# Merging input projection and recurrence preparation, with the convolution as matmuls and modulation by contraction quarters

## The reference, cut to what matters

```
# block 1
u = rmsnorm(x) * gain * (1 + sc_mix) + sh_mix
p = u @ w_in                                   # 2816 columns = 22 tiles of 128
y = p[:, 0:512] * sigmoid(p[:, 512:1024])      # tiles 0-3 and 4-7
y_conv = silu(layernorm(causal_depthwise_conv31(y) + b))
xs = p_r + mu * (shift_by_one(p_r) - p_r)      # the other 14 tiles: r, k, v (4 each), w|a, g
decay, a, gate = low-rank products of xs[w], xs[a], xs[g] with sigmoids
y_rwkv = recurrence(r, k, v, decay, a)         # 8 heads of 64, a state of 64 x 64 each
x += gt_mix * (concat(y_conv, y_rwkv) @ w_out)
x += gt_ffn * peer_ffn(modulated norm of x)    # top-16 of 16384 experts, 8 heads: row gather
x = rmsnorm(x)
# block 2: modulated norm, projections, two attentions, output, gated FFN
```

## Time and profile before

| | us |
|---|---|
| median of 3 runs | 1514.3 (1513.95 to 1515.32) |
| profiled execution | 1514.75 |
| its span, first to last instruction | 1512.5 |
| PE busy | 1257.1 (83%) |
| VectorE busy | 944.1 (62%) |
| ScalarE busy | 424.7 (28%) |
| input projection and convolution, 33 to 133 | PE 85.4, VectorE 74.7, ScalarE 30.5 busy |

### The profile page before, as it was taken

One profiled execution on the slowest core, in us unless ns is written; L12 is line 12 of the kernel. 1 busy time (PEld: TensorE's weight loads), 2 busy tenths in 40 slices (PEclk: granted clock), 3 DMA queues, 4 the chain that ended last, 5 costly groups with the idle time before them and its releaser, 6 DMA issues. The chain is left out here.

```text
span 1512.5 us, 19714 instructions
## 1 busy us (share of the span) xinstructions
PE 1257.1 (83%) x7650; PEld 860.7 (57%) x7650; DVE 944.1 (62%) x2121; ACT 424.7 (28%) x883; POOL 278.0 (18%) x263
## 2 busy tenths in 40 slices
PE   4996897784888788888888777887999778799988
PEld 2984585573424243333333222236998658799988
DVE  1696433347969787877878786567343867555443
ACT  3314222452111111111101010016355163544331
POOL 0000000002444444443434434310000000000000
PEclk8997898787999999999999999998999899899999
DMA  9545833843999999999999999974553034354443
GB/s 399 205 172 224 358 137 121 361 160 139 421 422 422 421 421 421 422 420 420 414 421 409 422 420 412 421 322 201 197 209 112 1 119 165 112 203 183 173 162 140
DMA packets 48188, 426.68 MB, mean 282 GB/s; under 512 B 5344, under 2 KB 5472, under 8 KB 5600
## 3 DMA queue, kind: packets, MB, share of 16 engines
q0 software_dynamic: 36864, 268.45, 42.9%
q1 hardware_dynamic: 11232, 156.98, 26.9%
HBM read 424.36 MB, written 1.05 MB: 281 GB/s over the span
## 5 line engine op out<-in xcount | busy, mean ns | idle before, releaser
L1298 PE MATMUL bank<-arena 128*128 128x512 f32 x1024 | 499.1, 615 | 129.5 <-DVE arena L1441 129.2
L1298 PEld LDWEIGHTS bank<-arena 128*128 128x128 f32 x1024 | 176.6, 190 | 437.0 <-DVE arena L1441 285.8
L1479 DVE CUSTOM_DVE_ANT_0 arena<-arena 128x1024 f32<-128x1024 f32 x256 | 313.5, 1224 | 149.3 <-DMA arena<-experts_in,arena 145.0
L1225 POOL DMA_INDIRECT arena<-experts_in,arena x256 | 277.4, 1084 | 589.5 <-PE bank L1298 349.9
L467 PE MATMUL bank<-rounded,rounded 128*128 128x256 f32 x1144 | 335.0, 293 | 44.5 <-DVE rounded L430 36.3
L469 PE MATMUL bank<-rounded,ring_r 128*128 128x256 f32 x1144 | 328.5, 287 | 0.0
L468 PE MATMUL bank<-rounded,rounded 128*128 128x256 f32 x1144 | 327.3, 286 | 0.0
L444 DVE TENSOR_TENSOR ring_r<-ring,rounded 128x1024 fp32r<-128x1024 f32 (+2 forms) x137 | 171.8, 1267 | 142.5 <-ACT rounded L439 142.4
L467 PEld LDWEIGHTS bank<-rounded,rounded 128*128 128x128 f32 x1144 | 222.7, 195 | 49.0 <-issue 27.8
L468 PEld LDWEIGHTS bank<-rounded,rounded 128*128 128x128 f32 x1144 | 223.9, 196 | 3.0 <-issue 2.9
L469 PEld LDWEIGHTS bank<-rounded,ring_r 128*128 128x128 f32 x1144 | 223.4, 195 | 0.0
(11 more groups left out here) (255 smaller groups left out, 993.8 us busy)
## 6 DMA issues: line engine op xcount, KB each, us to landing
ring<-slots_in SPq DMA_DIRECT2D x73, 2048.0 KB, 8.5
arena<-experts_in,arena POOLq DMA_INDIRECT x256, 13.6
xT<-xT_in SPq DMA_DIRECT2D x1, 1024.0 KB, 10.7
mixT<-slots_in SPq DMA_DIRECT2D x1, 1024.0 KB, 6.4
out_dram<-xT SPq DMA_DIRECT2D x1, 1024.0 KB, 3.9
con<-consts_in SPq DMA_DIRECT2D x1, 552.0 KB, 8.7
vec<-vecs_in SPq DMA_DIRECT2D x1, 167.0 KB, 2.3
```

The source lines that it names most:

```text
L1225: pool.indirect_dma_start(rows[:, r % GRING, :], None, experts_in, bass.IndirectOffsetOnAxis(ap=expert[:, tt, at:at + 1], axis=0)).then_in ...
L1298: ins = pe.matmul(psum[2 * tt + half][:, :], diag[:, r % DIAGS, :], rows[:, r % GRING, D + 512 * half:D + 512 * half + 512], start=(h == 0 ...
L1479: dve.tensor_tensor_reduce(rows[:, r % GRING, 0:D], rows[:, r % GRING, 0:D], utok[:, tt, :], 1.0, 0.0, ALU.mult, ALU.add, hdot[:, r:r + 1] ...
```

## The change

The order of the slots changes, and block 2's modulation leaves the recurrence. Old and new:

```
- ("ada", 4), ("w_in", 6), ("ada2", 2), ("lora", 1), ("ada3", 6), ("mod2", 12), ("w_out", 2), ("w_q", 4),
- ("w_in2", 10), ("rope", 1), ("gates", 2), ("w_br", 2), ...
+ ("ada", 4), ("w_in", 1), ("lora", 1), ("w_in_b", 5), ("convw", 1), ("ada_b", 8), ("w_out", 2), ("w_q", 4),
+ ("w_in2", 10), ("gates", 1), ("mod2b", 4), ("gates_b", 1), ("mod2c", 4), ("w_br", 2), ...
+ KEYS_AT, ROPE_AT, EARLY_ROWS = NSLOTS, NSLOTS + 1, NSLOTS + 2
```

**Modulation.** A slot now holds a quarter of the contraction (256 rows) for 2048 columns; six groups. `pe_mod(pe, g, first, last)` does the slices k from first to last:

```
+ for k in range(first, last):
+     ...
+     for j in range(4):
+         ins = pe.matmul(psum[MOD_BANK[g]][32 * j:32 * j + 32, :], csil[:, which, k, :],
+                         w[:, 2048 * (k % 2) + 512 * j:2048 * (k % 2) + 512 * j + 512],
+                         start=(k == 0), stop=(k == KT - 1))
+     if k % 2: ...            # frees the slot
+ def pe_mod_cols(pe, g):      # 4 products for 2048 columns, a 4-column piece of the identity as moving operand
```

**One block for projection and preparation.** The 14 recurrence tiles come first, in the order w|a, g, k, r, v, and are split (`buffers=4`); then b and a, plain. The preparation's steps are set between:

```
+ ORDER_IN = (12, 13, 4, 5, 6, 7, 0, 1, 2, 3, 8, 9, 10, 11)
+ if i == 4: lora_products()       # PE, after tile i
+ elif i == 6: gate_products()
+ elif i == 8: ... head_sums(5, bv, rw["ss"])
+ elif i == 15: ... head_sums(3, T2, rw["bonus"])

+ win.dve_lo(dve, 5)               # VectorE
+ win.dve_lo(dve, 6)
+ dve.wait_ge(rw["sigw"], CT)
+ for ct in range(CT): dve.tensor_tensor_scan(T3[:, ct, :], ...)
+ win.dve_lo(dve, 7)
+ shift(4, 6, 4)
+ win.dve_lo(dve, 8)
+ shift(6, 8, 6)
+ ...
```

**Convolution.** In the recurrence block SyncE first copies `ypad` to four time-shifted copies in SBUF (24 transfers, rows of 284 elements): partitions 32 b + ch of channel group b at shifts 0 to 3. A new slot `convw` holds diagonal weights. For each channel tile 32 products, two times between the steps of chunk 2, two times of chunk 3; ScalarE evicts with the bias:

```
+ for r in range(8):
+     for b in range(4):
+         ins = pe.matmul(psum[6 + ct % 2][32 * b:32 * b + 32, 0:T], w[:, b, ct, r, :],
+                         taps(b, ct)[:, 4 * r:4 * r + T], start=(r == 0), stop=(r == 7))
```

More of the change, by code:

```diff
@@ new lines, in build, with pe_mod @@
+        EARLY_AT = ARENA - GRING * 2 * D
+        early = area(EARLY_AT, 4, SLOT)
+        mrow = area(ARENA - 512, 512)
+        mrow_early = area(10752, 512)
+        def pe_mod(pe, g, first, last):
+            which, slots = GV[g]
+            for k in range(first, last):
+                if slots is None:
+                    if k % 2 == 0:
+                        pe.wait_ge(early_loaded[k // 2], 16)
+                    w = early[:, k // 2, :]
+                else:
+                    if k % 2 == 0:
+                        wait_slot(pe, slots[k // 2])
+                    w = ring[:, slots[k // 2] % RING, :]
+                for j in range(4):
+                    ins = pe.matmul(psum[MOD_BANK[g]][32 * j:32 * j + 32, :], csil[:, which, k, :],
+                                    w[:, 2048 * (k % 2) + 512 * j:2048 * (k % 2) + 512 * j + 512],
+                                    start=(k == 0), stop=(k == KT - 1))
+                if k % 2:
+                    if slots is None:
+                        ins.then_inc(early_used, 1)
+                    else:
+                        free_slot(ins, slots[k // 2])
@@ new lines, in act_mod @@
+        def act_mod(act, g):
+            slots = GV[g][1]
+            if slots is None:
+                act.wait_ge(early_used, 4)
+            else:
+                act.wait_ge(slot_used[slots[3] % RING], slots[3] // RING + 1)
+            if g:
+                act.wait_ge(gv_col, g)
+            act.copy(mrow_early if slots is None else mrow, psum[MOD_BANK[g]][:, :]).then_inc(gv_out, 1)
+        def pe_mod_cols(pe, g):
+            pe.wait_ge(gv_out, g + 1)
+            row = mrow_early if GV[g][1] is None else mrow
@@ L263, in pe_mod, with dve_mod @@
[L263 to L269, removed]
+        def dve_mod(dve, g):
+            dve.wait_ge(gv_col, g + 1)
+            cols, bias = slice(16 * (g % 3), 16 * (g % 3) + 16), ("ada_b", "b_mod_2")[g // 3]
+            return dve.tensor_tensor((mod1, mod2)[g // 3][:, cols], psum[MOD_BANK[g]][:, 0:16], vcol(bias, 16 * (g % 3), 16),
+                                     ALU.add)
@@ L752, in build @@
+        CONV = SLOTS["convw"][0]
+        NTAP_DMA = 4 * 6
+        mean, var, squares = area(7182, T), area(7438, T), uT[:, 0:CT, :]
         PM = [area(768 * c, 2, CT, C) for c in range(NC)]
@@ L1140, in build @@
         eight = [(i // 4, (i % 4) * P) for i in range(8)]
[L1141 removed]
+        residual_block("o1", "w_out", eight, mixT, mod1[:, 16:24], (after("ada_b"), after("w_out")), 0, early_rows=True)
         if STOP == "w_out":
@@ L1733, in build, with _ @@
         with nc.Block() as block:
+            @block.sync
+            def _(sp):
+                load_slots(sp, after("mod2b"), after("gates_b"))
             @block.tensor
@@ L1806, in _ @@
             def _(sp):
-                load_slots(sp, after("w_in2"), after("gates"))
+                load_slots(sp, after("gates_b"), after("mod2c"))
             @block.tensor
@@ L1896, in _ @@
             def _(sp):
-                load_slots(sp, after("gates"), after("w_br"))
+                load_slots(sp, after("mod2c"), after("w_br"))
             @block.tensor
@@ L2049 @@
         tiles(s + 5 + j, wi[:, 2120 + j * 512:2120 + (j + 1) * 512])
-    fill("gates", wi[:, 2120 + 5 * 512:])
+    tiles(SLOTS["gates"][0], wi[:, 2120 + 5 * 512:2120 + 6 * 512])
+    tiles(SLOTS["gates_b"][0], wi[:, 2120 + 6 * 512:])
     consts, rope = shape_constants()
-    slots[SLOTS["rope"][0]] = rope
+    slots[ROPE_AT] = rope
     tiles(SLOTS["w_br"][0], w["w_br_dsa_2"][0])
```

708 lines of the change are left out of this document (363 added, 345 removed).

## The result

| | us |
|---|---|
| before, median of 4 runs (range) | 1514.1 (1510.6 to 1515.3) |
| changed, median of 4 runs (range) | 1449.9 (1448.9 to 1454.2) |
| ratio (95% interval) | 0.9585 (0.956 to 0.961) |
| forecast (range) | 1450 (1434 to 1470) |

The account below looks back on a forecast made before the run. DMA bounds the gather; in the 262 us of stretches before it no engine is full. Terms -52.3 - 17 - 6.5 + 4 + 7 = -64.8 take the profiled 1514.75 us to 1450, range 1434 to 1470.

Parts of the forecast that it names:

- Merged block: Input projection, convolution and recurrence preparation as one block set by PE, with 7 us of stalls: 123.7 us against 176.0, -52.3.
- rival (a): Merged block starves PE: split tiles wait for low halves queued behind preparation, pauses bring half clock; up to +14, 1464; chance 0.21.
- Recurrence, -17: Recurrence up to w_out: pieces of 20, 44 and 38 us, 102 in all where it was 119.
- conv stretch: Middle of the recurrence: four convolution tiles at 3.7 us come, 3.8 us of modulation go, additions count in full; 44 us.
- Tables, -6.5: One table set for Ln and Exp saves 1.28 us loads: two before each FFN, one after the gather.
- Gather 0: Four early slots load beside the w_out stage, their last read ending before POOL's first gather: 0, up to +5.
- Rotary, +4: End of the rotary stage: quarter 4's slot lands late, so the stage ends at 1194 us; +4 (0 to +8).
- Attention, +7: Attention loop: eight modulation slices of 0.93 us and the column turn, a little hidden; +7 (+2 to +11).
- Late stages, -2.6: Branch products, output and second FFN: two table loads fewer before the second FFN, -2.6 us.
- Rival (b): Clock stays full, slices fall into gaps: recurrence 96 us, attention +2, merged block saves 3; 1436; chance 0.12.
- Rival (c): Table sets are loaded as before: +6.5, and about 2.6 in the recurrence's tail; 1459; chance 0.04.
- rival (d): Convolution's four column groups run one after another at half clock, 27.5 us a tile: 1545, 1490 at full clock; chance 0.03.

Follow-up runs that it names:

- again: The changed kernel run once more with no edit: 1449.5 us, ratio 0.9572 against the kernel before.
- low7_first: Changed kernel with VectorE making the low half of tile 7 before its wait for the eight sigmoids: 1450.9 us, ratio 0.9579 against the kernel before.
- halves_early: Changed kernel with each low half from 7 on ahead of the preparation step before it, first head sums behind tile 9: 1446.5 us.
- root_user_as_before: Changed kernel with VectorE's multiplication of chunk 1 by its root back in its old place, behind H3 of chunk 2: 1452.2 us.
- slot_behind_copies: Changed kernel with the 2 MB slot at the merged block's end issued behind the 24 shifted copies, not ahead of them: 1445.6 us.

## Why the prediction was right

The time was right (1450 for 1449.9 and 1449.5), and by its main terms for the reasons given. That it met the median to 0.1 us is luck: single executions lie 5 us apart, errors of several us cancel, and profile against profile the change is -60.1 (-62.4 with "again") for -64.8. No run undoes the merged block, the convolution as matmuls or the new modulation by itself; their shares rest on the stage times. Of the parts, only the table set was taken out alone.

- **Merged block, -52.3: measured -51.9.** PE sets the end, with 6.0 us of stalls for the 7 forecast. The cause was given as a list of pinches, the sigmoids first. The list was right in kind (low halves queue behind other steps of VectorE), but the first pinch alone is worth nothing (low7_first). All together are an order that can be undone (halves_early), so rival (a)'s mechanism was there at 6 us; its half clock was not (0.96 to 1.00 in the split tiles, and 1.00 behind them).
- **Recurrence, -17: measured -16.1, by two errors against each other.** The first 20 us took 26.3, with PE's stands of 0.90, 1.03 and 3.97 us in them. The forecast's 20.9 held one stand of 1.98 already, so some 4 us are new; the copies were named only as to when they land. The conv stretch of 44 us took 38.7. Its tile was right (3.6 for 3.7), but "what is added counts in full" was not: 33 - 3.8 + 14.4 gives 43.6. About 2 us of each error is only a boundary: the first piece has 544 records of recurrence products where the kernel before had 480 up to 203 us, and the conv stretch 764 for 811. The other 3 us lay in time that the chain had spare, though the earlier trace rows has PE busy 31.6 of 33 there: the records overlap, and per record a recurrence product went from 0.036 to 0.032 us of the stretch. That busy time did not show a full array here. The last stretch, 38, took 38.0. The stall behind the root (VectorE 7.07 us, then PE 4.94) was credited to the reordering; root_user_as_before shows no gain from that here: with the user back in its old place VectorE waits 4.66 us, and the recurrence is no longer. A likely reason, not shown, is that PE has slices to do in that time.
- **Tables, -6.5: measured -4.7 before and behind the first FFN** (forecast -3.9), and the second FFN's first product 1.3 us sooner behind Ln. Against a kernel with the change's other parts, the set is worth 18.6 (16.2 between the profiles). The forecast priced the set by the kernel before; the changed kernel's roots would load twice each, and four of them stand in the tail.
- **Gather 0:** the FFN's norm to the first gather took 31.4 us in the changed kernel and in the experiments with the set, so the early slots hold nothing up there. It is 3.5 us less than before, where the two loads make 2.6; what makes the rest is open.
- **Rotary, +4: +4.3**, and its cause, quarter 4's slot, is shown by taking it away. Index +0.2 for 0.
- **Attention, +7: +5.2 (5.9 in "again").** A slice costs 0.93 less what it hides: two rounds grew by 1.2 us, not 1.9.
- **Late stages, -2.6: +0.9 (-1.0 in "again"), and +1.5 in the input products.** The 2.6 of the tables did come: from the stage's first ScalarE step to its first product the second FFN took 8.7 us before and takes 6.1. They are used up by what no term had, the 0.04 us more for each split tile (2.88 for 2.84): the stretch from that first product to the end takes 206.7 us for 204.7 at the same mean clock of 0.97. The input products' +1.5 has the same sign and about the same share of its time. Its cause stays open. In the branch and output stage, where the instructions are the same, the granted clock differs (0.92 before, 0.89 after, 0.91 in "again").

Rival (b) was half true: the clock in the recurrence is 0.98 where it was 0.89, and attention grew by less than 7. But the recurrence took 103 us and not 96, and what the conv stretch gained is not the clock's, which was 1.00 there before the change too. Rival (c) is refuted for the changed kernel: no load stands between Ln and Exp. So is rival (d): a convolution tile takes 3.6 us at full clock.

## What to carry to other kernels

Ahead of an engine that sets the pace, put what it waits for first in the feeder's queue, all of it: one step moved gave nothing, all seven, with the head sums behind them, began the recurrence 5.9 us sooner with the same work. Put fillers where the profile shows idle time and one per gap: eight slices in eight consecutive rounds cost 5 us, and under 1 us with copy and column turn when each had a gap of its own. A 2 MB load that isn't needed for 80 us can still cost 4 us by its moment of issue, here together with 24 small copies.

## What the hardware showed that I had not expected

- PE stood 3.4 to 4.0 us with no releaser, in ten traces, while a slot and 24 copies shared the DMA engines (share 0.96 to 1.07 in three pieces from 124.3 to 138.8 us), and not with the copies alone (share 0.58 from 123 to 144 us). The first four copies, of 142 KB, took 8.4 us to land with the slot and 3.3 without it.
- The 24 copies need 19.8 us of SyncE to issue, 0.83 us each (18.3 and 0.76 in slot_behind_copies); the forecast had 0.4, which is what one of SyncE's first issues takes in the kernel before (0.38 to 0.43).
- 5.9 us gained early became 4.0 in the profile and 3.0 in the median: half clock (0.50) lasted about 17 us behind the same work instead of about 7. Four kernels with the same attention code had this longer stretch. Single edits of a few us should be read by stage first.
- The same split products start 0.120 us apart instead of 0.118 in the late stages of every kernel with the change, at the same granted clock.
